# Two-model kernel: the odd layer's mixer in another order of work

## Chip, cores and metric

One core of a Trainium2 chip (trn2). The metric is device time in microseconds of one launch, the median of several runs. Engines are named as in the profile: PE is TensorE, DVE VectorE, ACT ScalarE, POOL GpSimd; SP issues the weight loads.

## The reference

Two models run one after the other on 256 tokens of width 1024 in float32; each has two layers. The change touches the first model's layer 1, its "odd" mixer, cut here to what matters:

```python
cq, ckv, kr, ik, iw = _split(h @ w_in, (512, 256, 64, 64, 8))
cq, ckv = _rms_norm(cq, q_norm), _rms_norm(ckv, kv_norm)
qf = (cq @ w_qb).reshape(B, T, 8, 128 + 64)          # per head: 128 plain, 64 rotated
q_abs = einsum('bthd,chd->bthc', qf[..., :128], w_uk)   # "absorbed" into the latent space
qa = concatenate([q_abs, rope(qf[..., 128:])], -1) * (128 + 64) ** -0.5
kv_cat = concatenate([ckv, rope(kr)], -1)
qi = rope_first_32((cq @ w_iq).reshape(B, T, 8, 64)); ki = rope_first_32(layer_norm(ik))
isc = einsum('bqh,bqhs->bqs', iw * c, relu(einsum('bqhd,bsd->bqhs', qi, ki)))
idx = top_k(where(causal, isc, NEG), 64)             # 64 keys per token
pr = masked_softmax(einsum('bqhc,bqkc->bqhk', qa, kv_cat[idx]))
o_lat = einsum('bqhk,bqkc->bqhc', pr, ckv[idx])      # 256 numbers per head
y = einsum('bthc,chv->bthv', o_lat, w_uv).reshape(B, T, 1024) @ w_out
```

`_rms_norm` divides every number of a token by one number, the token's root mean square, and multiplies by a gain for each channel.

## The kernel before

All matrices are float32, channels on partitions and the 256 tokens along the free axis. Weights come through a ring of 12 slots of 512 KB (a unit is a slot's content, eight 128x128 blocks, or 128 rows of 1024); SP refills a slot once PE has added to `freed`. Products go to PSUM, eight banks of 512 numbers. Each engine has a program of its own, written out in order, and the programs meet at counters: `Steps.mark(label)` raises one, `Steps.at(label)` is what another engine waits for. So the order in the odd mixer is set by the order of the code in `odd_tensor`, `odd_scalar` and `odd_vector`.

`odd_tensor` (PE) goes like this. It forms eight tiles of 128 channels x 256 tokens (four of cq, two of ckv, the rotated key kr, the index key ik); `copy_tile` empties even tiles by ACT (L1459) and odd ones by DVE (L1461) into SBUF. Then come the index weights `iw` (L2051 with 8 columns), and sums of squares over channels by a product with a matrix of ones, after DVE has squared cq and ckv (L2222, `sq`). ACT takes the root (L2186), DVE the reciprocal of 512 numbers (L2232) and six multiplications (L2235, L2238): `cqn`, `ckvn`. The wait for step `cqn` stands ahead of all query products (`queries`, L1444: eight units of two tiles, four index tiles, four rotated, eight plain). Between them stand two `swap` products, which exchange halves for the rotation that DVE then does (`rotate`, L2256 to L2260), and in two groups of four the index products `index(h)`, each followed by a relu on ACT (L2198) and a weighted addition on DVE (`weigh`, L2272).

The absorbed products `q_abs` are 16 more tiles of the same stream (`ODD_TILES = 40`). DVE empties the odd ones, one in each of its eight rounds of top-k (`MAX8` L2295, `MATCH_REPLACE8` L2298), after the key rotation (`rotate(0, "c", ...)`) and the copy of the transposed latent (L2288). The rounds end in a mask `sel` that is added to the scores.

The attention has 16 units (head, token tile `tt`), `MLA_UNITS`, with 128 keys for `tt` 0 and 256 for `tt` 1, and runs as a pipeline over passes i: PE makes the scores of unit i, transposes the weights of unit i-2 (L1508) and makes the values of unit i-3; DVE adds the mask (L2313), takes the maximum (L1534, L1536) and weights the exponents of i-1 (L1543, L1548); ACT does the exponent (L1517) and the copy of the transposed weights (L1527). Scores use four PSUM banks in turn. The values of both tiles of a head share bank 6, which DVE copies to `o_lat` (L2322) before the next head's values. `up(h)` multiplies by w_uv, and ACT copies to `cat` (L2214). After the last head `out_projected` (L333, L351) makes the output rows: eight units of w_out, each with four products of 512 columns, first all of token tile 0, then of tile 1. The layer norm of tile 0 follows as soon as its rows are done. GpSimd has nothing to do in the odd mixer.

## Time and profile before

| | us |
|---|---|
| median of 3 runs | 2267.57 |
| lowest and highest of them | 2259.58 and 2275.94 |
| the profiled execution | 2258.09 |
| its span, first to last instruction | 2256.3 |
| its mean granted clock of TensorE | 0.967 |

A row of the timeline reads: start in us from the span's first instruction, duration, engine, line, operation, what is written and read, how many were merged, and in brackets how long the engine was idle before and who ended that. In the chain a row "547.25 13.81 PE psum L249 x64" is 64 matmul instructions in a row. Each product of the program appears as two matmul instructions.

### The profile page before, as it was taken

Reading aid. Unit: us, or ns where it says so; the run is one execution under the profiler, and the core shown is the slowest. Engines: PE = TensorE matmul, PEld = TensorE weight load, DVE = VectorE, ACT = ScalarE, POOL = GpSimd, SP = SyncE. Lnnn points to the kernel's source line nnn. Section 1 sums busy time; section 2 is a strip of 40 time slices with the busy share of each in tenths; the row PEclk is TensorE's granted clock in tenths of the full one; section 3 lists DMA queues with packets and bytes.
Section 4 is the critical chain, followed back from the end, with each engine's and each line's share of the span. In section 5 each row is a group of like instructions: output and inputs, shape, how many; then the busy total and the mean of one; then the engine's idle time right before and its main releaser. Section 6 shows DMA issues by size and latency. Waiting matters only on the chain.

```text
span 2256.3 us, 24984 instructions
## 1 busy us (share of the span) xinstructions
PE 2174.6 (96%) x9634; PEld 1577.1 (70%) x9634; DVE 489.9 (22%) x1059; ACT 336.7 (15%) x772; POOL 137.2 (6%) x156
## 2 busy tenths in 40 slices
PE   8978999999878999999999999999999999999998
PEld 6855666667655666667777877777777778867776
DVE  1336300021553000210001743000200016530001
ACT  1113200011121000120002531000200024410001
POOL 0000010010000100100000440000000002500000
PEclk9965999999989999999999999999999999999999
DMA  7410354444202544444444403444554434125443
GB/s 282 155 38 0 113 167 154 153 149 149 75 29 95 196 156 149 149 151 157 149 155 144 140 20 129 161 151 156 197 173 151 150 129 161 46 85 168 149 155 115
DMA packets 82883, 304.75 MB, mean 135 GB/s; under 512 B 9265, under 2 KB 9393, under 8 KB 82417
## 3 DMA queue, kind: packets, MB, share of 16 engines
q1 hardware_dynamic: 80496, 294.92, 39.0%
q0 software_dynamic: 2304, 8.65, 1.0%
q8 instruction: 62, 1.02, 0.2%
q14 instruction: 21, 0.16, 0.0%
HBM read 302.22 MB, written 1.05 MB: 134 GB/s over the span
## 4 chain that ended last, share of the span: by engine, by line
PE 93%; DVE 4%; ACT 1%; issue 1%; DVEq 1%; DMA 0%; ACTq 0%; SPq 0%
PE psum L249 41%; PE psum L381 23%; PE psum L648 6%; PE psum L1566 5%; PE psum L333 5%; PE psum L322 3%; PE psum L309 3%; PE psum L2051 3%; PE psum L1444 1%; PE psum L290 1%; PE psum L2366 1%; PE psum L1508 1%; DVE space L1914 0%; DMA ring<-in_weights 0%; DVE space L2322 0%
## 5 line engine op out<-in xcount | busy, mean ns | idle before, releaser
L249 PE MATMUL psum<-h,ring 128*128 128x256 f32 x4256 | 941.3, 379 | 7.0 <-DMA ring<-in_weights 7.0
L249 PEld LDWEIGHTS psum<-h,ring 128*128 128x128 f32 x4256 | 809.2, 190 | 167.8 <-issue 63.9
L381 PE MATMUL psum<-ring,hid 128*128 128x512 f32 x816 | 366.8, 592 | 0.0
L381 PEld LDWEIGHTS psum<-ring,hid 128*128 128x128 f32 x816 | 155.0, 190 | 151.6 <-issue 146.4
L451 DVE TENSOR_TENSOR hid<-psum,hid_act 128x256 f32<-128x256 f32 x102 | 43.3, 425 | 879.6 <-ACT hid_act L434 879.6
L434 ACT ACTIVATE hid_act<-psum 128x256 f32<-128x256 f32 x152 | 58.2, 383 | 1140.8 <-PE psum L249 1086.2
L381 PE MATMUL psum<-ring,space 128*128 128x512 f32 x400 | 175.4, 592 | 0.0
L381 PEld LDWEIGHTS psum<-ring,space 128*128 128x128 f32 x400 | 75.2, 190 | 85.3 <-issue 83.2
L309 PEld LDWEIGHTS psum<-h,ring 128*128 128x128 f32 x704 | 80.5, 192 | 4.1 <-issue 2.9
L309 PE MATMUL psum<-h,ring 128*128 128x128 f32 x704 | 81.7, 275 | 0.0
L322 PE MATMUL psum<-h,ring 128*128 128x128 f32 x704 | 80.1, 275 | 0.0
L322 PEld LDWEIGHTS psum<-h,ring 128*128 128x128 f32 x704 | 79.3, 192 | 0.0
L451 DVE TENSOR_TENSOR space<-psum,hid_act 128x256 f32<-128x256 f32 x50 | 21.2, 425 | 260.8 <-ACT hid_act L434 260.8
L1300 POOL TENSOR_TENSOR space<-space 128x256 f32<-128x256 f32 x90 | 70.0, 778 | 29.4 <-ACT space L928 16.6
L1566 PE MATMUL psum<-space 128*64 128x128 f32 (+7 forms) x276 | 64.4, 393 | 1.9 <-DVE space L1905 1.0
L648 PE MATMUL psum<-ring,cat 128*128 128x512 f32 x128 | 65.1, 636 | 0.0
L1566 PEld LDWEIGHTS psum<-space 128*64 128x64 f32 (+3 forms) x276 | 45.8, 222 | 21.2 <-issue 12.5
L2051 PE MATMUL psum<-space 128*128 128x128 f32 (+3 forms) x224 | 44.5, 354 | 15.8 <-DVE space L2322 12.7
L333 PE MATMUL psum<-ring,cat 128*128 128x512 f32 x120 | 52.0, 594 | 1.8 <-DVE cat L2014 1.3
L1444 PE MATMUL psum<-space,ring 128*128 128x256 f32 x160 | 41.1, 413 | 12.1 <-DVE space L1461 7.0
L333 PE MATMUL psum<-ring,h 128*128 128x512 f32 x120 | 51.8, 592 | 0.0
L2051 PEld LDWEIGHTS psum<-space 128*128 128x128 f32 (+1 forms) x224 | 34.3, 220 | 25.1 <-ACT space L1527 14.2
(330 smaller groups left out, 1388.8 us busy)
## 6 DMA issues: line engine op xcount, KB each, us to landing
ring<-in_weights SPq DMA_DIRECT2D x552, 512.0 KB, 3.3
space<-in_rows POOLq DMA_DIRECT2D x8, 512.0 KB, 8.4
space<-in_gains POOLq DMA_DIRECT2D x6, 512.0 KB, 4.1
const<-in_consts SPq DMA_DIRECT2D x1, 1493.0 KB, 11.0
h<-in_x SPq DMA_DIRECT2D x1, 1024.0 KB, 4.9
x<-in_x_tok SPq DMA_DIRECT2D x1, 1024.0 KB, 15.3
out<-x SPq DMA_DIRECT2D x2, 512.0 KB, 2.7
space<-in_params POOLq DMA_DIRECT2D x2, 509.5 KB, 7.3
```

Source lines behind the costliest of these rows:

```text
L249: last = pe.matmul(out, unit[:, i, :], rhs[:, i, :], start=(i == 0), stop=(i == KD - 1), skip_group_check=True)
L309: ins = pe.matmul(out[:, half(0)], unit[:, i, :], k.h[:, i, half(0)], start=(i == 0), stop=(i == KD - 1), skip_group_check=True)
L322: last = pe.matmul(out[:, half(1)], unit[:, i, :], k.h[:, i, half(1)], start=(i == 0), stop=(i == KD - 1), skip_group_check=True)
L333: ins = pe.matmul(k.psum[:, 2 * tt + b, :], lhs(j)[:, half(tt)], unit[:, b * 512:b * 512 + 512], start=first and j == 0, stop=last and j = ...
L381: last = pe.matmul(k.psum[:, 2 * tt + b, :], hidden_tile(k, held, f, tiles, gated)[:, half(tt)], unit[:, b * 512:b * 512 + 512], start=(f ...
L434: act.activation(k.hid_act[:, f % 2, :], k.bank(hidden_bank(f, gated))[:, 0, :], ACT.Silu if gated else ACT.Relu).then_inc(k.act_ready, 1)
L451: dve.tensor_tensor(hidden_tile(k, held, f, tiles, gated), k.bank(hidden_bank(f, gated))[:, int(gated), :], k.hid_act[:, f % 2, :], ALU.mu ...
L648: return pe.matmul(out, lhsT, rhs, start=start, stop=stop, skip_group_check=True)
L1300: pool.tensor_tensor(s.zd[:, tile, :], s.zd[:, tile, :], s.product[:, t % PRODUCTS, :], ALU.add).then_inc(s.product_added, 1)
L1444: last = pe.matmul(out, unit[:, part, :], rhs, start=(i == 0), stop=(i == len(products) - 1), skip_group_check=True)
L1566: return pe.matmul(out, lhsT, rhs, start=start, stop=stop, skip_group_check=True)
L2051: return pe.matmul(out, lhsT, rhs, start=start, stop=stop, skip_group_check=True)
```

## The change

All of it is in the odd mixer.

- The query norm factor is one number for each token. The queries are now formed from cq times the channel gain alone; the factor (`q_std`, by products of the squares with one column of ones, so tokens lie on partitions) is multiplied into the index weights `wi` and into the scale of the exponent (`q_scale`). The tiles are squared and scaled as they leave PSUM: even ones by ACT, odd ones by DVE.
- The order on PE: index key sums between the first query units; all eight `index` products together, the second swap behind the sixth query unit, the last two query units behind that. The absorbed products no longer belong to the tile stream (`ODD_TILES = 24`): each head's two go to one bank, which ACT copies.
- The key rotation moves to GpSimd (`odd_pool`), with ACT copying the swapped halves out of PSUM, and the copy of the transposed latent moves to ACT.
- Attention runs by token tile: all heads of tile 0, then all of tile 1. Scores have two banks (2, 3), since banks 0 and 1 collect output rows of tile 0. ACT copies the latent output after every unit. The up-projections are done for four heads at once in passes 8, 12, 16 and behind the loop; DVE copies them. The output rows of tile 0 stand inside the loop in passes 10, 11 and 13 to 18; those of tile 1 follow the loop.

```diff
-        return self.k.psum[:, u % 4, 0:self.branches * n].rearrange("p (b n) -> p b n", n=n)
+        bank = self.score_banks[u % len(self.score_banks)]
+        return self.k.psum[:, bank, 0:self.branches * n].rearrange("p (b n) -> p b n", n=n)
...
-        if u >= 4:
-            pe.wait_ge(self.f.att_exp, self.before + u - 3)
+        deep = len(self.score_banks)
+        if u >= deep:
+            pe.wait_ge(self.f.att_exp, self.before + u - deep + 1)
...
-                                  bias=self.f.bias[:, u % 4, b:b + 1], scale=self.scale,
+                                  bias=self.f.bias[:, u % 4, b:b + 1], scale=self.scale_of(tt),
...
-MLA_UNITS = [(h, tt) for h in range(8) for tt in range(2)]
+MLA_UNITS = [(h, tt) for tt in range(2) for h in range(8)]
+NSA_SCORES, NSA_TURNED = (0, 1, 2, 3), (4, 5)
+MLA_SCORES, MLA_TURNED = (2, 3), (4, 5)
+UP_SLOTS, ROW_SLOTS = (8, 12, 16), (10, 11, 13, 14, 15, 16, 17, 18)
...
-    if t < 24:
-        return f.qn[:, t - 16, :]
-    return f.q_abs[:, t - 24, :]
...
-ODD_TILES = 40
+    return f.qn[:, t - 16, :]
+
+
+ODD_TILES = 24
...
+    out_of_psum(6)
+    for tt in range(2):
+        for i in range(4):
+            mm(k.psum[:, 0, 16 + tt:17 + tt], k.sq[:, i, half(tt)], k.c("ones")[:, 0:1], i == 0, i == 3)
+    for i in range(2):
+        last = mm(k.bank(1)[:, 0, :], k.c("ones"), k.sq[:, 4 + i, :], i == 0, i == 1)
+    last.then_inc(*f.ope.mark("sums"))
...
-    pe.wait_ge(*f.odve.at("cqn"))
-    queries(4)
+    queries(1)
+    pe.wait_ge(k.odd_out, (EVEN_TILES + 8) // 2)
+    mm(k.bank(2)[:, 0, :], k.c("block64"), f.ik[:, 0, :]).then_inc(*f.ope.mark("ik_sum"))
+    queries(1)
+    pe.wait_ge(*f.odve.at("ik_sq"))
+    mm(k.bank(3)[:, 0, :], k.c("block64"), k.sq[:, 6, :]).then_inc(*f.ope.mark("ik_ss"))
+    queries(1)
     out_of_psum(12)
+    pe.wait_ge(*f.oact.at("std"))
     pe.wait_ge(*f.odve.at("ikn"))
     swap("swap_i", f.ri, "swap32")
     queries(2)
     pe.wait_ge(*f.odve.at("rope_i"))
-    for h in range(4):
-        index(h)
-    queries(1)
-    for h in range(4, 8):
+    for h in range(8):
         index(h)
     queries(1)
     out_of_psum(16)
     pe.wait_ge(*f.oact.at("r7"))
     swap("swap_c", f.rc, "swap64")
+    queries(2)
...
-    out_of_psum(24)
-    for i in range(2):
-        pe_tiles(k, pe, w, [[(h * 2 + c, f.qn[:, 4 * i + h, :])] for h in range(4) for c in range(2)])
     out_of_psum(ODD_TILES)
...
+    for h in range(8):
+        if h % 4 == 0:
+            wt = pe_take(k, pe, w, P)
+        if h >= 4:
+            pe.wait_ge(*f.oact.at(f"absorbed{h - 4}"))
+        for c in range(2):
+            last = mm(k.bank(4 + h % 4)[:, c, :], wt[:, h % 4 * 2 + c, :], f.qn[:, h, :])
...
+        last.then_inc(*f.ope.mark(f"absorbed{h}"))
+
+    pe.wait_ge(*f.oact.at("absorbed7"))
+    pe.wait_ge(*f.opool.at("rope_c"))
...
     def att_values(u, h, tt):
         pe.wait_ge(f.att_copied, 16 + u + 1)
-        if tt == 0 and h > 0:
-            pe.wait_ge(*f.odve.at(f"lat{h - 1}"))
+        if u > 0:
+            pe.wait_ge(*f.oact.at(f"lat{u - 1}"))
...
-    for i in range(16 + 6):
+    up_units, out_rows = [], []
+
+    def up(tt, group):
+
+        n = 2 * tt + group
+        if n == 0:
+            up_units.extend(pe_take(k, pe, w, P) for _ in range(2))
+        pe.wait_ge(*f.oact.at(f"lat{8 * tt + 4 * group + 3}"))
+        if n > 0:
+            pe.wait_ge(*f.odve.at(f"up{n - 1}"))
+        for j in range(4):
+            for c in range(2):
+                last = mm(k.psum[:, 7, j * P:j * P + P], up_units[group][:, j * 2 + c, :],
...
+        if tt == 1:
+            w.owed += 1
+        last.then_inc(*f.ope.mark(f"up{n}"))
+
+    def row(i, tt):
+
+        if i % 4 == 0:
+            pe.wait_ge(*f.odve.at(f"up{2 * tt + i // 4}"))
+        if tt == 0:
+            out_rows.append(pe_take(k, pe, w))
+        for b in range(2):
+            last = mm(k.psum[:, 2 * tt + b, :], k.cat[:, i, half(tt)], out_rows[i][:, b * 512:b * 512 + 512], i == 0,
+                      i == KD - 1)
+            if tt and i and b == 0:
+                pe_hand_back(k, w, last)
+        if tt:
+            w.owed += 1
+        return last
+
+    for i in range(16 + 3):
         if i < 16:
             att_scores(i, *MLA_UNITS[i])
+        if i in UP_SLOTS:
+            up(*divmod(UP_SLOTS.index(i), 2))
+        if i in ROW_SLOTS:
+            last = row(ROW_SLOTS.index(i), 0)
         if 2 <= i < 18:
             att.pe_turn(pe, i - 2, MLA_UNITS[i - 2][1])
-        if 3 <= i < 19:
+        if i >= 3:
             att_values(i - 3, *MLA_UNITS[i - 3])
-        if i >= 5 and i % 2 == 1 and i < 21:
-            up((i - 5) // 2)
-    pe.wait_ge(*f.oact.at("up7"))
-    out_projected(k, pe, w, border(0, 1, LN1))
+    last.then_inc(k.y_done, 1)
+    row(0, 1)
+    up(1, 1)
+    for i in range(1, KD):
+        if i == KD - 1:
+            pe_turn_h(k, pe, border(0, 1, LN1), 0, k.h_tok)
+        last = row(i, 1)
+    last.then_inc(k.y_done, 1)
...
+    for t in (0, 2, 4):
+        act.wait_ge(k.proj_ready, EVEN_TILES + t + 1)
+        src = k.bank(4 + t % 4)[:, 0, :]
+        act.activation(k.sq[:, t, :], src, ACT.Square)
+        act.activation(odd_tile_out(f, t), src, ACT.Identity, scale=f.p("q_norm", t) if t < 4 else 1.0).then_inc(
+            k.even_out, 1)
+    copy(6)
...
+    act.activation(f.wi, k.psum[:, 0, 0:16].rearrange("p (t h) -> p t h", t=2), ACT.Copy, scale=WI_SCALE)
+    act.activation(f.q_std, k.psum[:, 0, 16:18], ACT.Sqrt, bias=k.eps(LN_EPS), scale=1.0 / 512)
+    act.activation(k.std[:, 0, :], k.bank(1)[:, 0, :], ACT.Sqrt, bias=k.eps(LN_EPS), scale=1.0 / 256).then_inc(
         *f.oact.mark("std"))
...
+    copy(18)
+    act.wait_ge(*f.ope.at("swap_c"))
+    swapped = k.psum[:, 0:3, :].rearrange("p b (n t) -> p (b n) t", t=T)
+    for i, n in ((0, 2), (2, 2), (4, 1)):
+        last = act.activation(k.tmp[:, i:i + n, :], swapped[:, i:i + n, :], ACT.Copy)
+    last.then_inc(*f.oact.mark("swapped"))
+    copy(20)
+    copy(22)
+    act.wait_ge(*f.ope.at("turned"))
+    act.activation(f.ckv_tok, k.bank(3), ACT.Copy).then_inc(*f.oact.mark("turned"))
+    for h in range(8):
+        act.wait_ge(*f.ope.at(f"absorbed{h}"))
+        act.activation(f.q_abs[:, 2 * h:2 * h + 2, :], k.bank(4 + h % 4), ACT.Copy).then_inc(
+            *f.oact.mark(f"absorbed{h}"))
...
+        if i >= 3:
+            u = i - 3
+            act.wait_ge(f.att_out, 16 + u + 1)
+            act.activation(f.o_lat[:, MLA_UNITS[u][0], :, :],
+                           k.psum[:, 6, 0:2 * P].rearrange("p (c t) -> p c t", c=2), ACT.Copy).then_inc(
+                *f.oact.mark(f"lat{u}"))
...
+    for t in (1, 3, 5):
+        dve.wait_ge(k.proj_ready, EVEN_TILES + t + 1)
+        out = odd_tile_out(f, t)
+        dve.tensor_copy(out, k.bank(4 + t % 4)[:, 0, :])
+        dve.drain()
+        last = dve.tensor_tensor(k.sq[:, t, :], out, out, ALU.mult)
+        if t < 4:
+            dve.drain()
+            last = dve.tensor_scalar(out, out, f.p("q_norm", t), None, ALU.mult)
+        last.then_inc(k.odd_out, 1)
...
-    dve.reciprocal(k.rstd, k.std)
-    dve.drain()
-    for i in range(4):
...
-    last.then_inc(*f.odve.mark("cqn"))
+    dve.reciprocal(k.rstd[:, 0, :], k.std[:, 0, :])
+    dve.reciprocal(f.q_std, f.q_std)
+    dve.drain()
+    for tt in range(2):
+        dve.tensor_scalar(f.wi[:, tt, :], f.wi[:, tt, :], f.q_std[:, tt:tt + 1], None, ALU.mult)
+    dve.tensor_scalar(f.q_scale, f.q_std, C_SCALE, None, ALU.mult).then_inc(*f.odve.mark("q_scale"))
...
+    copy(19)
     diag = lambda x: x.rearrange("p (n t) -> p n t", n=3)[:, 0:3:2, :]
     dve.tensor_tensor(diag(f.isc), diag(f.isc), bc(k.c("causal_qk"), 2), ALU.add)
-    rotate(0, "c", f.rc, 16)
-    dve.wait_ge(*f.ope.at("turned"))
-    dve.tensor_copy(f.ckv_tok, k.bank(3)).then_inc(*f.odve.mark("turned"))
+    dve.drain()
...
-        tiles_out(25 + 2 * r, 26 + 2 * r)
+        if r in (2, 4):
+            copy(19 + r)
...
+        if i in UP_SLOTS:
+            up(UP_SLOTS.index(i))
+    up(3)
+
+
+def odd_pool(k, f, pool):
+
+    pool.wait_ge(*f.oact.at("swapped"))
+    pool.wait_ge(k.odd_out, (EVEN_TILES + 16) // 2)
+    pool.tensor_tensor(f.rt, f.rc, bc(f.cos[:, 0, :], 5), ALU.mult)
+    pool.tensor_tensor(k.tmp[:, 0:5, :], k.tmp[:, 0:5, :], bc(f.sin[:, 0, :], 5), ALU.mult)
+    pool.drain()
+    pool.tensor_tensor(f.rc, f.rt, k.tmp[:, 0:5, :], ALU.add).then_inc(*f.opool.mark("rope_c"))
```

How it moves instructions on PE, first behind the index weights. Line 2051 of before and 2063 of now is the helper `mm`, L1444 and L1446 are the query products. Before:

```order
L2051 MATMUL psum<-sq,const 128x256 [waits odd_elementwise]
L2051 MATMUL psum<-sq,const 128x256 x5
L2051 MATMUL psum<-space,const 128x256
L2051 MATMUL psum<-sq,const 128x256 [waits odd_elementwise]
L1444 MATMUL psum<-space,ring 128x256 [waits even_out,ring_filled2,odd_elementwise]
L1444 MATMUL psum<-space,ring 128x256 x3
L1444 MATMUL psum<-space,ring 128x256 [waits odd_out]
L1444 MATMUL psum<-space,ring 128x256 x3
```

Now:

```order
L2063 MATMUL psum<-const,sq 128x1 [waits odd_out,even_out]
L2063 MATMUL psum<-const,sq 128x1 x7
L2063 MATMUL psum<-sq,const 128x256 x2
L1446 MATMUL psum<-space,ring 128x256 [waits even_out,ring_filled2]
L1446 MATMUL psum<-space,ring 128x256 x3
L1446 MATMUL psum<-space,ring 128x256 [waits odd_out]
L1446 MATMUL psum<-space,ring 128x256 x3
L2063 MATMUL psum<-space,const 128x256 [waits odd_out]
L1446 MATMUL psum<-space,ring 128x256 [waits even_out,ring_filled3]
L1446 MATMUL psum<-space,ring 128x256 x3
L1446 MATMUL psum<-space,ring 128x256 [waits odd_out]
```

The query products lost their wait for `odd_elementwise`, and the sums of the index key moved between them.

Inside the attention, the second token tile. L1508 and L1519 are the transposes. Before, one head's second half (scores, transposes, values, up-projection):

```order
L2051 MATMUL psum<-space 128x256 [waits attention_exp]
L2051 MATMUL psum<-space 128x256 x2
L1508 MATMUL psum<-const,space 128x128 [waits attention_copied,attention_prob]
L1508 MATMUL psum<-const,space 128x128
L2051 MATMUL psum<-space 128x128 [waits odd_elementwise,attention_copied]
L2051 MATMUL psum<-space 128x128
L2051 MATMUL psum<-space,ring 128x256 [waits odd_activations,odd_elementwise]
L2051 MATMUL psum<-space,ring 128x256
```

Now, two passes of the second tile:

```order
L2063 MATMUL psum<-space 128x256 [waits attention_exp]
L2063 MATMUL psum<-space 128x256 x2
L2063 MATMUL psum<-ring,cat 128x512 [waits ring_filled3]
L2063 MATMUL psum<-ring,cat 128x512
L1519 MATMUL psum<-const,space 128x128 [waits attention_copied,attention_prob]
L1519 MATMUL psum<-const,space 128x128
L2063 MATMUL psum<-space 128x128 [waits odd_activations,attention_copied]
L2063 MATMUL psum<-space 128x128 x3
L2063 MATMUL psum<-space 128x256 [waits attention_exp]
L2063 MATMUL psum<-space 128x256 x2
```

An output row (`psum<-ring,cat`) or four heads of up-projections stand between scores and transposes; the values wait for ACT's copy (`odd_activations`) instead of DVE's.

The end of the mixer on PE. Before:

```order
L2051 MATMUL psum<-space 128x128 [waits attention_copied]
L2051 MATMUL psum<-space 128x128 x3
L2051 MATMUL psum<-space,ring 128x256 [waits odd_activations,odd_elementwise]
L2051 MATMUL psum<-space,ring 128x256
L333 MATMUL psum<-ring,cat 128x512 [waits ring_filled6,ring_filled5,ring_filled7,ring_filled4,ring_filled8,ring_filled3,ring_filled9,ring_filled2,odd_activations]
L333 MATMUL psum<-ring,cat 128x512 x29
```

Now:

```order
L2063 MATMUL psum<-space 128x128 [waits odd_activations,attention_copied]
L2063 MATMUL psum<-space 128x128 x3
L2063 MATMUL psum<-ring,cat 128x512 [waits odd_elementwise]
L2063 MATMUL psum<-ring,cat 128x512
L2063 MATMUL psum<-space,ring 128x128 [waits odd_elementwise,odd_activations]
L2063 MATMUL psum<-space,ring 128x128 x7
L2063 MATMUL psum<-ring,cat 128x512 x6
L2063 MATMUL psum<-ring,cat 128x512 [waits odd_elementwise]
L2063 MATMUL psum<-ring,cat 128x512 x5
```

Before, all 32 output products followed the last up-projection; now 16 of them, with the last up-projection among them.

## Rows read from the trace of the kernel before

**Rows 1.** The page, part 1: busy time, share of the span, instructions.
```profile
PE 2174.6 (96%) x9634; PEld 1577.1 (70%) x9634; DVE 489.9 (22%) x1059; ACT 336.7 (15%) x772; POOL 137.2 (6%) x156
```

**Rows 2.** The chain that ended last, 495 to 745 us: start us, us, what.
```profile
547.25 13.81 PE psum L249 x64
561.06 3.49 PE psum L2051 x32
...
564.80 3.30 PE psum L2051 x14
...
569.06 3.30 DVE rstd L2232
...
574.96 16.53 PE psum L1444 x64
...
652.14 2.41 PE psum L2051 x14
...
699.18 26.02 PE psum L333 x60
725.20 0.87 PE psum L290 x8
...
727.79 5.39 PE psum L309 x48
```

**Rows 3.** Busy time by stretch: PE, PEld, DVE, ACT, POOL, granted clock, DMA share, GB/s.
```profile
200.00:204.00 4.00, 4.00 (x16) 2.46 (x14) 2.64 (x9) 1.61 (x8) 0.00 (x0) 0.50 0.01 4
...
572.00:576.00 4.00, 1.04 (x3) 0.86 (x4) 3.92 (x8) 0.00 (x0) 0.00 (x0) 0.63 0.00 0
...
636.00:640.00 4.00, 4.00 (x11) 2.25 (x11) 1.51 (x6) 0.79 (x4) 0.00 (x0) 0.50 0.00 0
...
653.00:698.00 45.00, 33.48 (x188) 26.11 (x187) 17.96 (x59) 10.00 (x39) 0.00 (x0) 0.96 0.14 47
```

**Rows 4.** Timeline, 561 to 653 us: start us, us, engine, what, idle before.
```profile
602.62 2.43 DVE L2272 SCALAR_TENSOR_TENSOR space<-space 128x128 f32<-128x128 f32 x6
...
620.36 1.65 PE L1444 MATMUL psum<-space,ring 128*128 128x256 f32 x4 [4.49 <-DVE space L1461]
...
622.26 0.62 DVE L2295 MAX8 space<-space 128x8 f32<-128x128 f32 x2
...
624.13 0.62 DVE L2295 MAX8 space<-space 128x8 f32<-128x128 f32 x2
...
633.10 0.42 DVE L1461 COPY space<-psum 128x256 f32<-128x256 f32 x1
...
633.61 6.22 PE L2051 MATMUL psum<-space 128*128 128x128 f32 x18 [3.09 <-issue]
```

**Rows 5.** Timeline of one head of the attention, 652 to 660 us.
```profile
652.14 0.68 PE L2051 MATMUL psum<-space 128*128 128x128 f32 x4 [2.01 <-DVE space L2322]
...
654.59 0.30 DVE L2313 TENSOR_TENSOR psum<-psum,space 128x128 f32<-128x128 f32 x1 [2.60 <-PE psum L2051]
...
655.52 0.37 ACT L1517 ACTIVATE space<-psum,space 128x128 f32<-128x128 f32 x1 [3.69 <-DVE space L1536]
...
655.87 0.27 ACT L1527 ACTIVATE space<-psum 128x128 f32<-128x128 f32 x1
...
657.24 0.43 DVE L2313 TENSOR_TENSOR psum<-psum,space 128x256 f32<-128x256 f32 x1 [1.18 <-PE psum L2051]
...
658.43 0.47 ACT L1517 ACTIVATE space<-psum,space 128x256 f32<-128x256 f32 x1 [2.02 <-DVE space L1536]
...
658.75 0.68 DVE L2322 COPY space<-psum 128x512 f32<-128x512 f32 x1
...
659.58 0.68 PE L2051 MATMUL psum<-space 128*128 128x128 f32 x4 [2.02 <-DVE space L2322]
```

**Rows 6.** GpSimd by line, and GpSimd beside VectorE at 1293 us (timeline).
```profile
L2485 POOL TENSOR_TENSOR x<-x,space 128x1024 f32<-128x1024 f32 x8 | 16.0, 1996 | 3.9 <-issue 3.1
...
1293.22 0.73 POOL L1300 TENSOR_TENSOR space<-space 128x256 f32<-128x256 f32 x1 [0.16 <-issue]
1293.48 1.64 DVE L1168 SCALAR_TENSOR_TENSOR space<-space 128x256 f32<-128x256 f32 x2
```

228 lines of the change are left out of this document (94 added, 134 removed).

## The prediction

> **What bounds the kernel now.** I read four views, from the coarse to the fine. The page's first part says who works: TensorE is busy 96% of the span [rows 1], so only time in which it idles or runs at half clock can go, and it has to be looked for by stage. Second, the chain that ended last, cut to the odd mixer. It is TensorE nearly throughout, and its pieces show the stage's marks: the narrow products of the index weights start at 561.06 us, the sums of squares at 564.80, the first query product at 574.96, the output rows at 699.18, the MLP's first products at 727.79 [rows 2]. Third, the table by stretch with the granted clock: it is 0.63 at 572 to 576 us and 0.50, the lower of its two levels (1.2 of 2.4 GHz), at 636 to 640 [rows 3]. Fourth, the timeline, which shows the holes of TensorE and who ends them [rows 4, 5].
>
> The chain also prices the products. One call of the program is two matmul instructions here. A call with 128 columns is 5.39/24 = 0.225 us, with 256 columns 13.81/32 = 0.432, with 512 columns 26.02/30 = 0.867, with 8 columns 3.49/16 = 0.218 (so the weight side is the floor), a transpose 0.87/8 = 0.109 [rows 2]. Columns with 512 and 256 scale, narrow ones don't.
>
> There are three holes. (a) From the end of the sums, 564.80 + 3.30 = 568.10, to 574.96 the queries wait for the normed vectors; a reciprocal of 3.30 us lies in that chain, and only one call (0.43) is done meanwhile [rows 2]. (b) The absorbed products come after the second swap. They go through VectorE, which empties one bank in each round of the top-k (rounds start at 622.26 and 624.13, 1.87 us apart), and it must first do a rotation: TensorE stood still 4.49 us before 620.36, and its last wait ends with VectorE's copy at 633.10, so attention starts at 633.61 [rows 4]. (c) In attention each head takes 7.44 us, and TensorE waits 2.01 us of it for one thing, VectorE's copy of the latent output [rows 5]; the clock dips too (0.96 over 653 to 698) [rows 3]. The output rows come only when all this is over.
>
> **The change, part by part.** The odd mixer from 564.6 (the end of the index weights, 561.06 + 3.49) to 727.79 is 163.2 us. I rebuild that stretch.
>
> *Up to attention.* The query factor is a factor of a token, so it can be left out of the vectors and put on the index weights and in the exponent; the query products no longer wait for it. TensorE now has: 8 sums with one column, at the floor of the 8-column call, 8 x 0.218 = 1.7; 2 of 256 columns, 0.9; two for the index key, 0.9; 8 query units of 8 calls, 8 x 3.45 = 27.6; two swaps of two calls with 512 and one with 256 columns, 2 x (2 x 0.867 + 0.432) = 4.3; the transposes 0.4; the absorbed products 16 x 0.432 = 6.9. The index products of 8 heads stand together now. By columns they are 5.3 us, or 2.6 if the two row halves overlap, but heads 4 to 7 wait for the relu of heads 0 to 3, and these for the accumulations at 2.43/3 = 0.81 us a head [rows 4]: I take 4.2. One wait is new: attention waits for ScalarE's copy of the last absorbed head, which no row shows in this form. It lies between the 256-column copy, 0.37, and VectorE's 512-column copy, 0.68 [rows 5], plus a hand-over; I take 0.75. Sum 1.7 + 0.9 + 0.9 + 27.6 + 4.3 + 0.4 + 6.9 + 4.2 + 0.75 = 47.7, and attention starts at 564.6 + 47.7 = 612.3; I allow 0.2 and say 612.5, against 633.61 before. **First term: 21.1 us.**
>
> What must not come late for that. The index key: its two reciprocals (half the width of the one of 3.30, so about 1.7 each) and copies end near 578.3 us, when the third query unit ends, at 578.4: no slack, a few tenths at most. The mask: the index products start at 587.4 and the eight accumulations end near 595.6; a round without a copy is 1.87 less 0.42 of the copy [rows 4], 1.45, so eight rounds with two copies end near 609, masks near 610, and the copy after the fifth round, for which the absorbed products wait, near 604.7, when TensorE is at 604.6. The key rotation is on GpSimd, three operations of 1280 elements. A GpSimd operation of 1024 is 1.996 us [rows 6], so 2.5 each; at the rate of its 256-element ones, 0.73, it is 3.7 each. ScalarE's copies of the swap end near 598.8, so the rotation ends between 606.4 and 609.9: hidden by 2 us or more.
>
> *Attention.* The same units run as 8 of the first token tile, then 8 of the second. TensorE needs per unit of the first tile 3 x 0.225 + 0.11 + 2 x 0.225 = 1.24 us, of the second 3 x 0.432 + 0.22 + 4 x 0.225 = 2.42. An up-projection of four heads is 8 x 0.225 = 1.80, an output row for one tile 2 x 0.867 = 1.73.
> The first tile's units are bound by latency. From the mask's addition to the exponent's start it is 655.52 - 654.59 = 0.93 us, the exponent and the next copy together end at 655.87 + 0.27 [rows 5], that is 1.66 after the scores are ready; a hop, the values (0.45) and the scores after next (0.67) make 2.9 us for two units. So 1.45 to 1.5 a unit (VectorE's own work, 0.93 plus the weighting, is about as long). With only two score banks, scores wait for the exponent two units back, but that is 0.67 + 0.11 + 0.93 + 0.37 + 0.1 = 2.2 for two units: not the limit. Three units to fill at 5.3 us in all, and four at 1.5: the first eight passes end 11.2 us after the start.
> From the ninth pass TensorE has more work than latency. For the second tile the same loop is 1.30 + 0.11 + 1.19 (658.43 - 657.24) + 0.47 + 0.37 + 0.2 + 0.90 = 4.5 for two units, 2.3 a unit, below 2.42 and far below 4.15 with a row. Passes 9 to 19 are 3.66 (up), 1.86, 3.70 and 4.15 (row), 4.22 (up), three of 4.15, 4.65 (up and row), 2.85, 2.63: 40.2. Then one row, one up-projection, six rows, the transposes 0.87 and the last row: 1.73 + 1.80 + 10.4 + 0.87 + 1.73 = 16.5. Together 11.2 + 40.2 + 16.5 = 67.9, so the MLP starts at 612.5 + 67.9 = 680.4. Before it was 727.79 - 633.61 = 94.2. **Second term: 26.3 us.** Of the 67.9 TensorE's work is 65.2, so little is left to win.
>
> What is moved with it costs nothing by these rows. The latent output is copied by ScalarE for each unit (0.38), VectorE's copy for four heads (0.69) falls under rows. VectorE's last copy stands ahead of the layer norm of the first tile and starts it near 669 instead of 664.5, but its transposes are due only at 678. The rows hold 8 of 12 weight slots and the up units 2 until 668, then they come back at 1.73 us each while the first MLP products need four: two are loaded and three are freed at once, as now [rows 2].
>
> **Sum.** 21.1 + 26.3 = 47.4 us. The profiled execution took 2258.09 us (span 2256.3), so 2210.7 in its terms; the median of the three runs, 2267.57, is 9.5 above it, so 2220.2 in theirs. The changed kernel may be measured at either; I take 2217, a base of 2264.4, also for the rivals.
>
> A rule speaks against the move to GpSimd. Rows first: beside GpSimd's additions two VectorE operations with two SBUF inputs and 256 elements took 1.64 us, 0.82 each [rows 6], where three pairs of 128 and 256 elements without GpSimd took 2.43, so 0.81 for both together [rows 4]. The Trainium skill, page "SBUF — State Buffer", section "SBUF: two separate sides", states that VectorE and GpSimd share one port pair, which one operation locks for its whole length against a VectorE operation with two SBUF inputs. The trace agrees. During the rotation VectorE runs the top-k, whose operations read one tile, so I count nothing; rival 3 has the other case.
>
> **Rivals.**
> 1. *The clock falls in the fill of attention* (17%). TensorE works 3.4 of the first 5.3 us there. For: it fell after hole (a), and the attention of now holds only 0.96 [rows 3]. Against: three units only, and work without a pause before. Half clock over the eight first units and the first of the second tile makes them 2.4 instead of 1.5: 7 to 8 us lost. Gain 40, so 2224.
> 2. *The rows push the latency chain instead of filling its holes* (8%): each unit takes what it took (7.44 for two) and the rows are added after or between. Only the first term stays, with 2 us from a steady clock: gain 23, 2241.
> 3. *The shared port* (8%): the rotation's 7.6 us and VectorE's top-k exclude each other. The mask then comes at 617.6, scores wait some 4 to 5 us, and the bank copy before the absorbed products is late too: 5 to 7.6 lost, gain 41, 2223.
> 4. *Slower than before* (3%): the clock drops at the start of attention and stays low, as in the even mixer, where TensorE was busy all the time at 0.50 [rows 3]. The 65.2 us of work then take 130, the MLP starts at 743, 15 us later than before: 2280. It decides once the low clock covers more than 47 of these 65 us. Against: in this very stage the clock came back by itself (0.50 at 636 to 640, 0.96 over 653 to 698) [rows 3].
> 5. *The order doesn't come out so* (2%): some due time, the index key or a copy, makes TensorE wait in each step and the gain is under 22 us: about 2250.
>
> **How the numbers follow.** My forecast, 2217, has 62%, by itself 2207 to 2226 (the bound 2.7 us from idle to full work, the two bases 9.5 apart, and hand-overs I left out). The low end for all is full TensorE work on the faster base, 2258.1 - 52 = 2206, less a little: 2204. The high end takes in rivals 1 and 3 on the slow base, 2235, rounded to 2238, and leaves out rivals 4, 5 and most of 2. Under 1% can't be told from no change here; 1% faster is below 2245. Cases with that: forecast, 1, 3 and 2: 0.95 with a doubt taken off, 0.94; within 1%: rival 5 and that doubt, 0.03; slower 0.03.
>
> **What would show it.** Right: query products follow the sums without a hole, at 567 us; attention starts at 612 to 613; TensorE idles under 4 us from there to the MLP at 680; the clock row is 1.00 at 565 to 610; total busy time of VectorE unchanged. First term wrong: TensorE waits for the index key near 578, or for a bank near 605. Second term wrong: waits for the exponent or the turned copy in passes 9 to 19. Rival 3: top-k rounds longer than 1.5 us beside GpSimd. What breaks the forecast is a low clock after 612, or a hole over 5 us anywhere.

## The result, and the profile after

The changed kernel took 2232.64 us (median of 4 runs, 2229.96 to 2243.33), the kernel before 2263.57 on the same chip (4 runs): ratio 0.985, 95% interval 0.982 to 0.988. In a second comparison (6 runs against 11) it was 0.981, 0.979 to 0.984. So it is faster by 1.5 to 2%, 31 to 43 us on the medians. The forecast was 2217; the time lies in the given range, but above the likeliest case's own range (2207 to 2226), and most of the missing time has causes that can be named. That it still fell within the stated range is owed to the range's upper part, which rivals 1 and 3 on the slower base had set.

The page's first part, after [rows 1]:

```profile
PE 2175.9 (98%) x9674; PEld 1582.1 (71%) x9674; DVE 478.1 (21%) x1045; ACT 346.5 (16%) x788; POOL 145.2 (7%) x159
```

TensorE's busy time hardly changed (2174.6 before); the span is 25.6 us shorter. The idle time went. It went in the odd mixer, as the table for this one stretch shows, from the end of the index weights to the start of the MLP, first before (columns: stretch, length, then busy time and instructions of PE, PEld, DVE, ACT, POOL, granted clock, DMA share, GB/s):

```profile
564.55:727.79 163.24, 132.75 (x546) 91.76 (x547) 73.79 (x202) 30.06 (x91) 0.00 (x0) 0.92 0.18 61
```

and after:

```profile
572.75:702.19 129.44, 126.71 (x586) 92.59 (x587) 61.87 (x185) 40.08 (x105) 7.76 (x3) 0.93 0.21 76
```

TensorE stood still for 163.2 - 132.8 = 30.5 us of this stretch before and for 2.7 after. The stretch is 33.8 us shorter; 47.4 were forecast. The mean clock of the stretch is hardly better (0.93 against 0.92): of 126.7 us of busy time a part is still work at half speed. In time it is less, since the stretch is shorter: by stretches of 4 us about 27 us at the lower level before and 17 after. How much of the 33.8 us that is worth was not separated. Behind the stretch nothing changed: from the MLP's start to the end of the launch it is 2258.09 - 727.79 = 1530.3 before and 2232.6 - 702.19 = 1530.4 after.

The chain that ended last, after, cut to the same part [rows 2]:

```profile
569.28 7.28 PE psum L2063 x52
576.55 4.09 PE psum L1446 x16
...
615.40 7.17 PE psum L2063 x32
...
661.28 4.30 PE psum L2063 x18
...
682.29 17.31 PE psum L2063 x64
699.60 0.87 PE psum L290 x8
...
702.19 5.38 PE psum L309 x48
```

The first query unit follows the sums at 576.55, with no wait for normed vectors; the absorbed products stand at 615.40 and no longer go through VectorE. The first row holds 32 instructions of the index weights (3.47 us, so they end at 572.75) and the sums. Attention starts at 623.25, 50.5 us after the index weights; forecast 47.9, before 69.1. From there to the MLP it is 78.9 us; forecast 67.9, before 94.2. So the first term gained 18.6 us (forecast 21.1), the second 15.2 (forecast 26.3).

Two things are new. The timeline at the start of the attention, after:

```profile
623.25 2.18 PE L2063 MATMUL psum<-space 128*128 128x128 f32 x12 [0.69 <-ACT space L2267]
625.15 0.21 DVE L1547 TENSOR_SCALAR space<-space 128x1 f32<-128x1 f32 x1
625.44 1.28 ACT L1528 ACT_TABLE_LOAD   x1 [2.25 <-DVE space L1547]
626.74 0.46 ACT L1528 ACTIVATE space<-psum,space 128x128 f32<-128x128 f32 x1
627.34 1.13 PE L2063 MATMUL psum<-space 128*128 128x128 f32 x6 [1.91 <-ACT space L1528]
```

The third scores wait 1.91 us for the first exponential (two score banks), and that waits 1.28 us for its table, which ScalarE loads only once the first maximum is there. Below, "the hole" is this wait and "late table" this load. And the clock, after, in stretches of 4 us [rows 3]:

```profile
624.00:628.00 4.00, 2.09 (x13) 1.54 (x13) 2.07 (x8) 2.27 (x5) 0.00 (x0) 1.00 0.01 4
628.00:632.00 4.00, 4.00 (x19) 3.32 (x18) 2.33 (x10) 1.65 (x7) 0.00 (x0) 0.61 0.00 0
632.00:636.00 4.00, 4.00 (x16) 3.10 (x16) 1.22 (x6) 1.04 (x5) 0.00 (x0) 0.50 0.00 0
636.00:640.00 4.00, 4.00 (x17) 3.55 (x18) 2.10 (x10) 1.22 (x5) 0.00 (x0) 0.50 0.00 0
640.00:644.00 4.00, 4.00 (x18) 3.02 (x16) 1.34 (x6) 1.75 (x8) 0.00 (x0) 0.68 0.00 0
```

TensorE works 2.09 of 4 us, then the granted clock goes to its lower level for 13.7 us (each row's share at 0.50, by its mean, added up), and a unit of the first token tile takes 2.84 us instead of the 1.5 forecast. A busy time of 4.00 there is not full work; it is half speed. Below, such a time at the lower level is called a dip, with its length worked out in the same way.

### The profile page after: what moved, and what is told of

Its sections match the earlier page's. It is cut to its first block, busy times and chain, and to the rows that moved or that the text cites. A ratio compares the mean times of both kernels' runs of the same rounds, so it can differ in the third digit from the quotient of the medians.

```text
span 2230.7 us, 25069 instructions
## 1 busy us (share of the span) xinstructions
PE 2175.9 (98%) x9674; PEld 1582.1 (71%) x9674; DVE 478.1 (21%) x1045; ACT 346.5 (16%) x788; POOL 145.2 (7%) x159
## 4 chain that ended last, share of the span: by engine, by line
PE 95%; DVE 3%; ACT 1%; DVEq 0%; issue 0%; DMA 0%; ACTq 0%; SPq 0%
PE psum L249 41%; PE psum L381 23%; PE psum L648 7%; PE psum L1580 6%; PE psum L2063 4%; PE psum L322 4%; PE psum L333 3%; PE psum L309 3%; PE psum L1446 1%; PE psum L290 1%; PE psum L1519 1%; PE psum L2437 1%; DVE space L1928 0%; DMA ring<-in_weights 0%; DVE h L1184 0%
## 5 line engine op out<-in xcount | busy, mean ns | idle before, releaser
L381 PEld LDWEIGHTS psum<-ring,space 128*128 128x128 f32 x400 | 75.2, 190 | 85.3 <-issue 83.2
L1580 PE MATMUL psum<-space 128*64 128x128 f32 (+7 forms) x276 | 69.5, 416 | 1.9 <-DVE space L1919 1.0
L648 PE MATMUL psum<-ring,cat 128*128 128x512 f32 x128 | 64.3, 629 | 0.0
L648 PE MATMUL psum<-space 64*128 64x128 f32 (+5 forms) x536 | 51.0, 281 | 0.0
L648 PEld LDWEIGHTS psum<-space 64*128 64x128 f32 (+4 forms) x536 | 40.6, 169 | 10.0 <-issue 3.0
L928 ACT ACTIVATE space<-space 128x256 f32<-128x256 f32 x90 | 42.0, 505 | 14.7 <-POOL space L1300 14.4
## 6 DMA issues: line engine op xcount, KB each, us to landing
x<-in_x_tok SPq DMA_DIRECT2D x1, 1024.0 KB, 15.4
```

The source lines that it names most:

```text
L381: last = pe.matmul(k.psum[:, 2 * tt + b, :], hidden_tile(k, held, f, tiles, gated)[:, half(tt)], unit[:, b * 512:b * 512 + 512], start=(f ...
L648: return pe.matmul(out, lhsT, rhs, start=start, stop=stop, skip_group_check=True)
L928: act.activation(out, s.zs[:, tile, j:j + T], ACT.Identity, scale=s.p("cm_conv_w", tile * CMW + j)).then_inc(s.product_ready, 1)
L1580: return pe.matmul(out, lhsT, rhs, start=start, stop=stop, skip_group_check=True)
```

## The experiments

The runs were made in sets, each with its own executions of the kernel before, and times of different sets differ by some us. The part behind the MLP's start varies too: 1530.3 to 1539.4 us over the profiled executions of the changed kernel and its variants, with dips that come out longer or shorter (0.83 at 1300 to 1350 us in e10_hole, 0.93 in the changed kernel). So for effects of a few us the stretch is read and not the median. In each run I read two terms: the first from the end of the index weights to the first scores, the second from there to the MLP. In the second, the mark "fill" is the time until VectorE adds the mask to the first scores of the second token tile (21.04 us in the changed kernel, 12.5 in the forecast: 11.2 and 1.3 for these scores), and "rest" is what follows (57.9; forecast 55.4).

**The changed kernel again.**

> The changed kernel once more, unaltered. If the late clock of the even layer (0.50 from 228 to 244 us, odd mixer entered 8.2 us late) is chance of that one execution, the index-weights products end between 564 and 573 us, not again at 572.8, or the executions spread by some 8 us; if it belongs to the changed code it comes back at 572.8 within 0.5. The stretch from the end of the index-weights products to the start of the MLP should be 129.4 us again (within 1) and the clock should fall again to 0.50 in the first passes of the attention if it is this code that makes it fall; the rival, that this dip was chance as well, gives a stretch near 122.

2230.07 us. The query stage begins at 567.63 + 3.47 = 571.1. First term 52.2 (the dip at 572 to 580 was longer, 6.8 us instead of 3.4, and the first query unit took 5.16 us), second 76.6, fill 18.7, rest 57.9, the whole stretch 128.7 (129.4 within 1 expected). The clock fell again with the hole (here already at its end, 0.82 at 624 to 628), for 6.9 us instead of 13.7. So the fall comes back, but its length differs between two executions of one kernel. The entry into the odd mixer varies as well. The granted clock of the even mixer, code that the change doesn't touch, before:

```profile
224.00:232.00 8.00, 8.00 (x37) 5.39 (x37) 4.63 (x13) 2.26 (x8) 0.00 (x0) 0.73 0.00 1
232.00:240.00 8.00, 7.37 (x48) 5.06 (x47) 5.72 (x16) 4.37 (x14) 0.00 (x0) 1.00 0.01 2
```

and after:

```profile
224.00:232.00 8.00, 8.00 (x26) 5.34 (x26) 3.13 (x8) 1.51 (x5) 0.00 (x0) 0.50 0.00 0
232.00:240.00 8.00, 8.00 (x29) 5.51 (x29) 3.99 (x11) 3.02 (x10) 0.00 (x0) 0.50 0.00 1
240.00:248.00 8.00, 8.00 (x34) 5.50 (x33) 3.23 (x9) 2.10 (x6) 0.00 (x0) 0.59 0.01 2
```

The clock came back near 228 us in the one and 247 in the other. The index weights start at 561.06 before, at 569.28 after. Over the 13 profiled executions of the changed kernel and its variants this start lies between 561.1 and 571.4, ten times between 567.6 and 569.8. The profiled execution of before, at 561.06, was a lucky one: its time is 5.5 us and more under the medians of its kernel. So the profiled pair differs by only 25.5 us (33.8 less 8.2), while the medians differ by 31 to 43. That the other executions of before entered later is inferred from their times, since only one of them was profiled.

**Table load hidden** (e1_table).

```diff
     copy(10)
+    act.wait_ge(*f.odve.at("q_scale"))
     act.wait_ge(*f.ope.at("ik_ss"))
...
-    act.wait_ge(*f.odve.at("q_scale"))
     for i in range(16 + 3):
```

> ScalarE's wait for q_scale stands 20 us earlier, so that only one wait stands before the first exponential. Theory: the load of the exponential's table (1.28 us at 625.44) then runs ahead of the first maximum, in ScalarE's idle time, and the first exponential starts 1.3 us sooner: stretch 128.1 instead of 129.4, and if the shorter hole of TensorE (0.6 instead of 1.9 us) keeps the clock up, another 6 to 8 less. Rival: the load stays behind the wait for the maximum, since it is put directly before the activation, and nothing changes (129.4).

2226.62 us (2221.66 to 2235.69). ScalarE's timeline:

```profile
617.83 0.60 ACT L2268 ACTIVATE space<-psum 128x512 f32<-128x512 f32 x1 [0.27 <-PE psum L2063]
618.45 1.28 ACT L1528 ACT_TABLE_LOAD   x1
620.64 0.46 ACT L1528 ACTIVATE space<-psum,space 128x128 f32<-128x128 f32 x1 [0.91 <-DVE space L1547]
```

The load now runs directly behind the last copy, beside the first scores. With one wait ahead of the exponential it runs before that wait (so in all five variants with this edit: e1, e3, e8, e10, e11); with two waits in a row it ran behind the second (in the eight other executions). The hole is 0.58 us, the clock is 1.00 in every stretch of 4 us from 600 to 700, the second term is 73.3, fill 15.4, rest 57.9. So table and clock cost 5.7 us together, all in the fill. The stretch is 123.8 us, 5.6 shorter than the changed kernel's.

**Fillers in the holes** (e2_fill), and **both** (e3_both).

```diff
+    def filler(n):
+
+        for _ in range(n):
+            mm(k.psum[:, 7, 0:T], k.c("ident"), f.ckvn[:, 0, :])
+
     for i in range(16 + 3):
+        filler({0: 1, 2: 4, 3: 1, 4: 1}.get(i, 0))
         if i < 16:
```

> Seven products of 128x256 that write an unused bank (no result uses them, 0.43 us each at full clock) are put into TensorE's holes at the start of the attention: one before the first scores, four before the third, one before the fourth and fifth. Theory (TensorE's clock falls because of the holes between 618 and 630): the clock stays at 1.00 through 628 to 644, the units of tile 0 take 1.5 us instead of 2.84, stretch 122 to 124. Rival 1 (the latency chain over scores, maximum, exponential and transposes sets 2.84 us a unit, not the clock): 129.4 to 131. Rival 2 (the fall has its cause before 620 and cannot be averted here): 130 to 131, the clock again 0.50.

2221.09 us, four runs within 0.7 us; this profiled execution also entered the odd mixer early (561.13). The table is still late, but TensorE has work:

```profile
620.00:624.00 4.00, 4.00 (x26) 3.21 (x24) 2.50 (x11) 1.40 (x8) 0.00 (x0) 1.00 0.00 0
624.00:628.00 4.00, 3.66 (x25) 2.92 (x24) 2.33 (x10) 2.16 (x10) 0.00 (x0) 1.00 0.00 0
628.00:632.00 4.00, 3.66 (x23) 2.75 (x22) 2.33 (x10) 2.16 (x9) 0.00 (x0) 1.00 0.00 0
```

The clock stays at 1.00 (attention starts at 615.1 here), fill 17.6, second term 75.5: above the 73.3 of e1_table by 2.2 for the late table and the fillers together. I had expected the second term 5.4 to 7.4 shorter than 78.9; it was 3.5, so the clock was kept up, but half of the gain went into the fillers and the table.

> e1_table and the seven filler products of e2_fill together. Theory (holes make the clock fall): 1.00 throughout 600 to 700 us; the fillers hide in the short holes only in part, so second term 73 to 76 us. Rival (that the clock held in e1_table and e2_fill was chance): a window at 0.50 to 0.85 behind the start of the attention, 77 us or more.

2229.28 us. Clock 1.00 from 600 to 700, second term 75.2, fill 17.3. As for the clock the theory holds. But the fillers are then mere work: 1.9 us more than e1_table alone. Where the hole is gone, leave them out.

**The hole put back** (e10_hole): e1_table, and in VectorE's loop

```diff
             dve.wait_ge(f.att_scores, 16 + i + 1)
+            if i == 0:
+                dve.reciprocal(k.rstd[:, 0, :], k.std[:, 0, :])
```

> As e1_table (table load hidden, clock 1.00 there), but VectorE does one more reciprocal of 256 elements (about 1.65 us, its result is not changed by it) ahead of the first maximum, so that TensorE again has a hole of some 2 us at the start of the attention. Theory (such a hole makes the clock fall): second term 73.3 + 1.7 + 4 to 5 = 79 to 80 us, with 0.50 in the windows behind it. Rival (the fall is chance, or belongs to the table load only): 75 us and 1.00 throughout.

2238.67 us (2231.0 to 2238.84). The third scores wait 2.2 us again, and the clock falls again:

```profile
624.00:628.00 4.00, 1.78 (x11) 1.25 (x10) 3.07 (x7) 1.26 (x3) 0.00 (x0) 1.00 0.02 4
628.00:632.00 4.00, 4.00 (x19) 3.31 (x20) 2.50 (x13) 1.39 (x6) 0.00 (x0) 0.64 0.00 0
632.00:636.00 4.00, 3.66 (x24) 3.02 (x24) 2.39 (x11) 2.04 (x9) 0.00 (x0) 0.94 0.00 0
```

The second term is 75.8, 2.5 more than in e1_table: 1.6 for the larger hole, 0.9 for the clock. My number was too large, since the dip lasted only 3.4 us here; the rival's 75 lies nearer, but the rival had the clock at 1.00 throughout, and it fell. Set against e1_table, three executions with a like hole give a rough rate of 0.26 to 0.32 us for each us of dip: a dip of 13.7 us cost 4.4 (21.04 less 15.36 less 1.3 for the table), one of 6.9 us 2.0, one of 3.4 us 0.9. The median is 12 us above that of e1_table, far more than these 2.5 us: the profiled execution also entered 5.0 us later and took 6.9 us more behind the MLP's start.

Over all experiments: of the eight profiled executions with the hole of 1.4 to 3 us near the start of the attention seven show the fall behind it (the exception is e4_rows128, below); of the five whose holes there are all under 1 us (e1, e2, e3, e8, e11), none does. Hole and fall go together in 12 of 13, and putting the hole back brought the fall back, in one profiled execution. That the hole always brings it is not true, and what decides in e4_rows128 stays open.

**128 rows instead of 64** (e4_rows128); it adds a second head's rotary product to each head's scores.

```diff
-        mm(out, f.rc[rows, i, half(tt)], f.rc[rows, 4, 0:n], False, True)
+        mm(out, f.rc[:, i, half(tt)], f.rc[:, 4, 0:n], False, True)
```

> The rotary product of each head's scores takes all 128 rows of its tile instead of 64 (it adds a second head's product, so the scores are other ones; the same columns move). Theory: the 0.33 us of idle time of TensorE at the load of 64 rows goes, in each of the 16 passes, 4 to 5.3 us in all: passes of tile 1 take 4.2 instead of 4.52, stretch 124 to 125.5 where the clock is as before. Rival: the idle time belongs to the switch from tokens to scores and not to the number of rows: no change, 129.4.

2228.87 us. The weight loads of one pass of the second tile in the changed kernel:

```profile
661.01 1.63 PEld L2063 LDWEIGHTS psum<-space 128*128 128x128 f32 x12
662.97 0.29 PEld L2063 LDWEIGHTS psum<-space 64*128 64x128 f32 x2 [0.33 <-issue]
663.60 0.30 PEld L2063 LDWEIGHTS psum<-ring,cat 128*128 128x128 f32 x2 [0.33 <-issue]
```

and with 128 rows:

```profile
658.19 2.06 PEld L2063 LDWEIGHTS psum<-space 128*128 128x128 f32 x14
660.27 0.41 PEld L2063 LDWEIGHTS psum<-ring,cat 128*128 128x128 f32 x2
```

On both sides of the 64-row load the load queue stands for 0.33 us. With 128 rows this is gone. So the standing belongs to the change in the number of rows; why the engine does it, no run shows. The clock also stayed at 1.00 here, behind the same late table and a like hole, so the stretch is 121.2 us, less than either theory said, and the dip must be left out of the comparison: a pass with a row takes 4.13 us instead of 4.52 and the rest 55.0 instead of 57.9; my 55.4 for it left this out. The same columns move, so the loss isn't in the products.

**The rows of tile 0 out of the loop** (e5_rows_after), and **four score banks** with that (e6_banks4).

```diff
-UP_SLOTS, ROW_SLOTS = (8, 12, 16), (10, 11, 13, 14, 15, 16, 17, 18)
+UP_SLOTS, ROW_SLOTS = (8, 12, 16), ()
...
             att_values(i - 3, *MLA_UNITS[i - 3])
+    for i in range(KD):
+        last = row(i, 0)
     last.then_inc(k.y_done, 1)
```

> The eight output rows of the first token tile stand behind the 19 passes instead of inside them; all else as in the changed kernel. Theory: with a row a pass of the second tile is bound by TensorE (4.52 us, of which 1.73 for the row), without it by TensorE's 2.8 or the latency loop of about 2.3 to 2.5, so the rows cost nearly the same in either place: second term 79 us (77 to 82, the width is the clock's). Rival (the rows inside fill holes of the latency chain and are what the gain comes from): passes of 3.7 us as before the change, half of 7.4, and a second term of 86 us or more.

2234.43 us. Fill 21.04 as in the changed kernel, second term 80.4, so 1.5 more (77 to 82 expected, the rival 86 or more). A pass of the second tile without a row:

```profile
660.00 2.55 PE L2063 MATMUL psum<-space 128*128 128x128 f32 x14
662.48 0.44 PE L1519 MATMUL psum<-const,space 128*128 128x128 f32 x2
662.76 2.55 PE L2063 MATMUL psum<-space 128*128 128x128 f32 x14
```

It is 2.76 us long, 1.76 less than with a row (4.52), and the row is 1.73. The rows inside cost their own work and no more, and gain 1.5 us. Of these, 0.9 are waits for ScalarE's latent copy in the last two passes without rows (0.35 and 0.57). What takes the attention from 7.44 us for a head to 1.86 (a unit of the first tile in e1_table) + 2.76 is, by elimination, the order by token tile, with each unit's latent copy on an engine that is free, not the rows. Those two were changed together, and no run parts them.

> As e5_rows_after, with four banks for the scores instead of two, which the rows no longer hold. Theory: in the fill the third scores no longer wait for the first exponential (1.91 us at 625.43 in the changed kernel), so the fill is 1 to 2 us shorter, and the steady passes are alike: 1 to 2 us less than e5_rows_after, more only if the clock stays up. Rival (two banks bind every pass of the first tile): 0.3 us in each of 8 passes more, 4 us less than e5_rows_after.

With `MLA_SCORES = (0, 1, 2, 3)` on top: 2232.34 us, second term 77.5, fill 18.2. The third scores no longer wait, but the first transposes do (1.42 us for VectorE's weighting behind the same late table), and the clock falls, for 6.8 us where e5_rows_after had 13.7. Of the 2.9 us that it is better, 2.2 to 2.4 are the clock's by the figures above, so some 0.5 to 0.7 is left for the banks (an estimate): less than theory and rival said.

**The sums behind the first query unit** (e7_sums_later): the ten products of the sums stand after `queries(1)`.

> The eight one-column sums and the two of the latent vectors stand behind the first query unit instead of ahead of it. Theory (the clock's 0.78 at 572 to 580 comes from the wait for the squares and the one-column products that follow, worth 1.2 us at the sums and 0.6 at the first query unit): the sums then have their operands long since, attention starts 49 us after the end of the index weights instead of 50.5. Rival 1: the dip goes with the narrow products themselves and moves with them (50.5). Rival 2: the norm factors come 3.5 us later and TensorE waits for the index key near 588: 51 to 54.

2232.79 us. The timeline:

```profile
572.81 3.71 PE L1446 MATMUL psum<-space,ring 128*128 128x256 f32 x16
576.36 1.84 PE L2063 MATMUL psum<-const,sq 128*128 128x1 f32 x16
578.06 1.11 PE L2063 MATMUL psum<-sq,const 128*128 128x256 f32 x4
```

In the changed kernel the same four instructions with 256 columns take 2.06 us and the query unit behind them 4.09, here 1.11 and 3.57. The granted clock is 1.00 at 572 to 580 instead of 0.78. First term 621.78 - 572.95 = 48.8 (expected 49): 1.6 us of my error in this term. The other executions bear this out: the first term is 50.5 to 50.6 in all nine with 3.4 us at the lower level there, 52.2 in the two with 6.8 (a_again, e8_padded), 48.8 and 49.0 in the two with none (e7, e11). TensorE doesn't wait for the index key. The dip didn't move with the one-column products, so rival 1 falls. But the timeline of the changed kernel shows no wait of TensorE ahead of them either (index weights to 572.7, sums from 572.60), so my theory's wait isn't shown: what the run took away is that the one-column products follow directly on those with 8 columns. Which property of that sequence counts wasn't tried further.

**Key rotation back on VectorE** (e9_dve_rot), after the fifth top-k round.

> The key rotation is back on VectorE, after the fifth round of the top-k and its bank copy, all else as in the changed kernel. Its three operations of 1280 elements take 1.3 to 1.4 us each on VectorE by its other operations of 1280, some 4.1 us. Theory (GpSimd's part is worth only what VectorE lacks in slack, and the mask is ready 3.4 us before VectorE needs it): the first maximum comes 0.6 to 1.2 us later, second term longer by that and first term unchanged. Rival 1 (the move to GpSimd carries a good part of the gain): 4 us or more later. Rival 2 (port contention was paid in the changed kernel): the top-k rounds fall from 1.52 us and nothing is lost.

2235.48 us. VectorE adds the first mask in the changed kernel:

```profile
624.41 0.30 DVE L2377 TENSOR_TENSOR psum<-psum,space 128x128 f32<-128x128 f32 x1 [3.43 <-PE psum L2063]
```

and this run:

```profile
618.67 1.49 DVE L2364 TENSOR_TENSOR space<-space,tmp 128x1280 f32<-128x1280 f32 x1
...
625.45 0.43 DVE L2369 TENSOR_TENSOR space<-space,const 128x256 f32<-128x256 f32 x1
625.97 0.30 DVE L2383 TENSOR_TENSOR psum<-psum,space 128x128 f32<-128x128 f32 x1
```

The first mask is added 2.23 us after the attention's start (623.74) instead of 1.16: 1.07 us, as expected, and the first term is the same 50.5. The second term is 77.4, not longer but 1.5 shorter than in the changed kernel. But the dip lasted 6.8 us here instead of 13.7; with the 2.2 to 2.4 us of that put back (an estimate) it is 0.7 to 0.9 longer. The three operations are 4.4 us on VectorE and 7.8 on GpSimd (2.90, 2.45, 2.45), but on GpSimd they are hidden. In the changed kernel a round of the top-k beside them took 1.52 us (611.92 to 613.44), like the one ahead of them (606.62 to 608.14), so that round paid nothing for sharing.

**The parts that help, together.** e8_padded is e1_table with 128 rows, and the scores stay what they were: GpSimd writes the rotated key into two tiles that are zero in the other half of the rows, and the rotary product reads all 128 rows.

```diff
-        mm(out, f.rc[rows, i, half(tt)], f.rc[rows, 4, 0:n], False, True)
+        mm(out, f.rc[:, i, half(tt)], f.rk[:, h % 2, 0:n], False, True)
...
+    for part in range(2):
+        rows = slice(HEAD * part, HEAD * part + HEAD)
+        last = pool.tensor_copy(f.rk[rows, part, :], f.rc[rows, 4, :])
```

> As e1_table, and the rotary product of each head's scores takes 128 rows with the right result: GpSimd writes the rotated key twice into tiles that are zero in the other 64 rows (a fill of 512 elements and two copies of 256 more on GpSimd, some 2 us, which end before the attention starts). Theory: passes of the second tile 4.13 us instead of 4.52 and the first tile's units shorter too, second term 73.3 less 0.39 for each of 8 passes of the second tile and 0.1 to 0.3 for each of the first: 68 to 70 us, clock 1.00. Rival: GpSimd's additions come late and the attention starts up to 2 us later; or the clock falls as in e4_rows128's sisters: 73 to 75.

2223.28 us (2217.45 to 2231.37); second term 69.4 (68 to 70 expected), fill 14.4, rest 55.0, clock 1.00 in it. Its first term is 52.2, since the dip at 572 to 580 was longer here (0.57 and 0.58, so 6.8 us).

> e8_padded with the sums behind the first query unit (e7_sums_later) and two single filler products of 0.43 us in the fill (before the first and the third scores). Theory, every part adding up: first term 48.8, second term 68 to 70, so 117 to 119 us from the end of the index weights to the start of the MLP instead of 129.4; time 2219 to 2222 on the chip where the changed kernel takes 2230 to 2232. Rival (a hole elsewhere takes what is won, or the clock falls somewhere else): 122 us or more.

2222.4 us (2212.64 to 2229.47), 0.980 of before (0.976 to 0.983). The chain:

```profile
571.42 3.47 PE psum L2064 x32
574.89 3.57 PE psum L1447 x16
578.46 3.08 PE psum L2064 x22
...
673.78 17.31 PE psum L2064 x64
691.09 0.87 PE psum L290 x8
...
693.68 5.39 PE psum L309 x48
```

From 574.89 to 693.68 it is 118.8 us (expected 117 to 119), with attention starting at 623.86: first term 49.0, second 69.8. The stretch is 10.6 us shorter than in the changed kernel and only 3 from the forecast of 115.8. On the medians it is 8 to 10 us faster than the changed kernel; the intervals of the ratios meet, and this execution entered the odd mixer latest of all (571.42), so the stretch is the better evidence. It is faster than the kernel before (ratio 0.980); that it is faster than the changed kernel is shown by the stretch, not by the times.

## Why the prediction was right or wrong

**Right.** The three holes were the thing to win, and they are gone: TensorE's idle time in the stretch went from 30.5 to 2.7 us. No wait for normed vectors, none for VectorE in the absorbed products (the wait for ScalarE's last copy is 0.69 us; 0.75 forecast), none for the index key. The passes from the ninth on are bound by TensorE; the tail, from the end of the last values (684.74 + 0.90 in the timeline) to 702.19, is 16.55 us (16.5 forecast). Rivals 2, 3 and 5 fall: rows don't push the passes (e5), the top-k isn't slowed (1.52 with and without), and nothing came late. Rival 4, slower than before, did not happen: the dips ended by themselves. These parts are read from the waits in the traces; apart from the key rotation, the rows and the score banks, no part of the change was taken back alone, so what each is worth by itself is not shown.

Three of the signs I had named did not show. The clock row is not 1.00 at 565 to 610 but 0.78 and 0.79 at 572 to 580. Attention starts at 623.25, not at 612 to 613: 8.2 us are the late entry and 2.6 the first term. And VectorE's total busy time did not stay the same, it fell from 489.9 to 478.1, while ScalarE's rose by 9.8 and GpSimd's by 8.0.

**Rival 1 came true**, which I gave 17%: the clock fell in the fill. It is the step "three units only, and work without a pause before" that failed. I had TensorE working 3.4 of the first 5.3 us, and had seen the clock fall after hole (a); it fell in seven of eight executions with such a hole. Its size was 4.4 us (5.7 of table and clock, less 1.3) rather than the 7 to 8 I had priced. The dip behind such a hole lasted 13.7 us in three executions, 6.8 to 6.9 in three, 3.4 in one and was missing in one; this execution had one of the longest.

**Left out of the first term** (50.5 for 47.9): the clock at the sums, 1.6 us, shown by e7. The other 1 us is not traced to single steps.

**Left out of the second** (78.9 for 67.9), from the steps of e1 and e8:
- 1.3 us, ScalarE's table load. Before the change it was hidden; I counted the new wait for the query factor as free, since the factor is long ready. The wait cost nothing, but it moved the load.
- 4.4 us, the clock.
- 3.9 us, the 64-row loads: 2.9 in the rest, 1.0 in the fill (73.3 to 69.4). My 3 x 0.432 for the scores and 3 x 0.225 for the small ones priced calls of equal rows; the price of the change of rows isn't in a chain piece of like calls. The same products ran before the change, so this isn't a cost of the change but of my sum, which left no gap to hide it in.
- 1.5 us, what e8_padded has left over: its fill is 1.9 us longer than forecast (14.4 for 12.5; a unit of the first tile takes more than 1.5 us), its rest 0.4 shorter (55.0 for 55.4).

**The base.** I took 2264.4 between the profiled execution and the median. The medians of before in the four sets are 2263.6, 2272.8, 2272.8 and 2267.9: against the base the first is 0.8 us lower and the others 3.5 to 8.4 higher; the error of the mechanism is the one in the stretch, 33.8 instead of 47.4.

## What to carry to other kernels

Once the long waits are gone, look at the first microseconds of a stage: a hole of 2 us at a pipeline's start cost 0.9 to 4.4 us more here by a lower granted clock, so hide the latency of the first unit (a table load, a maximum) and only fill it with work for nothing if it can't be hidden. A wait that never waits can still move an instruction that the program doesn't write out (here the table load) behind it; put it where an earlier wait stands. And price matmul calls from a row where they alternate as they will in the new order, not from a run of equal ones.
